# Routing on the unscaled residual sum, a quiet start of the experts, and a last scatter in four column pieces, in a two-layer transformer encoder

## The chip, the cores and the metric

The kernel runs on one core of a Trainium2 chip. The metric is the device time of one execution in microseconds, lower is better; it is given as the median of several runs. Names of engines: PE (TensorE matmul), PEld (its weight loads), DVE (VectorE), ACT (ScalarE), POOL (GpSimd), SP (SyncE, which here only issues DMAs).

## The reference

Two sequences (512 prompt tokens and 1024 sample tokens, width 1024, float32) go through the same two-layer encoder. A layer adds an attention mixer to the residual, and then a routed mixture of experts. What matters here is everything between the mixer's output projection and the experts' sum:

```python
x = x + concat(attention outputs) @ w_out          # residual sum, called y below
h = x * rsqrt(mean(x*x) + 1e-6) * gain             # norm before the experts
aff = softmax(h @ w_router, axis=-1)               # 16 experts
gates, idx = top_k(aff.T, 2 * tokens / 16)         # each expert picks its tokens
hid = silu(h[idx] @ w_gate) * (h[idx] @ w_up)
x = x.at[idx].add(gates * (hid @ w_down))          # scatter-add onto the residual
```

Each expert takes 64 prompt tokens and 128 sample tokens. All large products are made from a high and a low part (three matmuls of float32r in place of one of float32).

## The kernel before, in words

The program is a chain of phases with a barrier between each two: all engines finish a phase, SP's waits for its last stores among them, before any starts the next. Per layer: attention phases, then `output_phase` (L1055), then `expert_phase` (L1423). The output phase of the first layer also merges three attention parts (ME, `merge_start` and `merge_end`); that of the second does not.

**Output phase.** The 1536 tokens are 12 tiles of 128 rows, in the order of ORDER (eight sample tiles, then four prompt tiles). The loop runs over steps s; in step s each engine works on tile s - lag for each kind of work:

- lag 0: the loads, and the merge on DVE and ACT. lag 1: `turn_o` on PE (8 transposes), the copy to the high part on ACT (L1189) and the low part on DVE (L1268). lag 2: `multiply` on PE, 48 matmuls of 512 columns into the one accumulator ps_y; part 0 is the first half and waits for y_ready of the tile before, since ps_y must have been read.
- lag 3: DVE reads ps_y and adds the residual (yb, L1252, "the y add"), ACT squares and sums (L1195), POOL makes the reciprocal root (rstd, L1173 and L1174), DVE makes the normed tile hb (L1276), PE turns it (`turn_h`, L1325), ACT copies it out (L1211), PE multiplies it with the router weights (`route`, L1333).
- lag 4: DVE takes the row maximum (L1255), ACT the exponential (L1198), DVE the reciprocal and the product (L1261, L1265), PE turns the 16 affinities (`turn_a`, L1343), DVE copies them into the table aff (L1290). From the eighth tile on DVE runs rounds of `choose` (L1046; a round is MAX8, FIND_INDEX8 and MATCH_REPLACE8) on the sample rows: 3, 3 and 2 rounds behind the affinity copies of three steps.

Every engine works its list in program order. PE's list of a step is the order written at L1349: turn_o, multiply part 0, turn_h, turn_a, multiply part 1, route. DVE's list (L1245): y add, maximum, merge_start, reciprocal and product, low part, hb, merge_end, affinity copy, choose. SP stores y and h and waits at the end for the last stores (L1165).

**Expert phase.** DVE runs 8 more rounds of choose (`TopK.vector`, L1383), PE turns the lists, DVE makes gate and idx. Then POOL issues two indirect gathers (xs of 128 rows, xp of 64 rows, 4 KB each; L1527 and L1529). Weights come in 192 chunks of 1 MB over a ring of six buffers; SP issues the next load when DVE has made the low part of a chunk (`low`, L1592; three of them ahead of the first expert, LOOK = 3). DVE waits for `asked`, which POOL sets when both gathers are issued, then makes these three low parts, then takes part in splitting the turned tokens (`x_out`, L1597). The last four chunks of an expert are the down projection; DVE writes the scaled result of each into 256 columns of cs and cp (`result`, L1603). When the fourth is there POOL copies the index columns (L1513, L1514) and issues two indirect accumulating DMAs onto y (`add`, L1511, L1516 and L1518), and waits for them.

## Time and profile before

| what | value |
|---|---|
| median of 3 runs | 4049.76 us (4045.23 to 4051.99) |
| the profiled execution's own time | 4044.71 us |
| its span, first to last instruction | 4042.9 us |
| PE busy | 3810.6 us, 94% of the span |
| DVE / ACT / POOL busy | 2674.3 / 2134.8 / 859.5 us |
| mean granted TensorE clock | 0.973 of full speed |
| DMA | 583.89 MB, mean 144 GB/s |
| output phase, first layer | from 1194.3 to 1403.6 us of the span |
| output phase, second layer | from about 2870 to 3069.6 us |

Times in the rows below are microseconds from the span's start. In the timelines a row is start, duration, engine, line, operation, output <- inputs, count, and in brackets how long the engine had been idle before it and what released it. The duration of a matmul is longer than the distance to the next one, since matmuls overlap; distances between starts are what counts. A granted clock of 1.00 is 2.4 GHz and 0.50 is 1.2 GHz. PE is busy for almost the whole span, so time is found in the stretches where it isn't, or at the half clock: the joints between phases, and the step order of the output phase.

### The profile page before, as it was taken

Reading aid. Unit: us, or ns where it says so; the run is one execution under the profiler, and the core shown is the slowest. Engines: PE = TensorE matmul, PEld = TensorE weight load, DVE = VectorE, ACT = ScalarE, POOL = GpSimd, SP = SyncE. Lnnn points to the kernel's source line nnn. Section 1 sums busy time; section 2 is a strip of 40 time slices with the busy share of each in tenths; the row PEclk is TensorE's granted clock in tenths of the full one; section 3 lists DMA queues with packets and bytes.
Section 4 is the critical chain, followed back from the end, with each engine's and each line's share of the span. In section 5 each row is a group of like instructions: output and inputs, shape, how many; then the busy total and the mean of one; then the engine's idle time right before and its main releaser. Section 6 shows DMA issues by size and latency. Waiting matters only on the chain. (4 is left out here: it accounts for less than half of the span.)

```text
span 4042.9 us, 75073 instructions
## 1 busy us (share of the span) xinstructions
PE 3810.6 (94%) x27032; PEld 3679.2 (91%) x27032; DVE 2674.3 (66%) x5509; ACT 2134.8 (53%) x3992; POOL 859.5 (21%) x1437
## 2 busy tenths in 40 slices
PE   7999999999979879999999979999895999999998
PEld 7989988999978679999999979999785999999998
DVE  5665664667664567777777747777535777777775
ACT  5554554566642245656565546555322555656654
POOL 5132220444420011111111123333000111111110
PEclk9999999999989889999999989999997999999999
DMA  3000001122124378887788721000335778777884
GB/s 99 17 21 8 23 17 35 45 67 64 55 95 149 128 222 254 249 253 238 247 247 255 237 86 47 31 24 14 142 134 180 232 253 251 247 237 251 254 245 124
DMA packets 487368, 583.89 MB, mean 144 GB/s; under 512 B 18032, under 2 KB 442480, under 8 KB 487152
## 3 DMA queue, kind: packets, MB, share of 16 engines
q1 hardware_dynamic: 470640, 522.40, 39.3%
q0 software_dynamic: 14336, 50.34, 5.8%
q10 hardware_dynamic: 2176, 8.39, 0.5%
q8 instruction: 122, 2.00, 0.2%
q14 instruction: 94, 0.77, 0.1%
HBM read 514.85 MB, written 66.21 MB: 144 GB/s over the span
## 5 line engine op out<-in xcount | busy, mean ns | idle before, releaser
L1594 DVE TENSOR_TENSOR wl<-raw,wh 128x2048 fp32r<-128x2048 f32 x384 | 879.0, 2290 | 277.5 <-ACT wh L1549 276.7
L1549 ACT CAST wh<-raw 128x2048 fp32r<-128x2048 f32 x384 | 732.7, 1908 | 23.1 <-DMA raw<-in_w_gate 20.7
L1691 PE MATMUL ps_g<-xT,wh 128*128 128x384 f32 x2048 | 599.4, 359 | 3.2 <-DVE xT L1600 3.2
L1691 PE MATMUL ps_u<-xT,wh 128*128 128x384 f32 x2048 | 594.8, 357 | 0.0
L1693 PE MATMUL ps_g<-xT,wl 128*128 128x192 f32 x2048 | 479.0, 254 | 0.0
L1693 PE MATMUL ps_u<-xT,wl 128*128 128x192 f32 x2048 | 477.1, 253 | 0.0
L151 PE MATMUL psP<-ring_high,hTh 128*128 128x384 f32 (+1 forms) x1344 | 463.8, 345 | 11.9 <-ACT V L669 5.4
L152 PE MATMUL psP<-ring_low,hTh 128*128 128x384 f32 (+1 forms) x1344 | 445.1, 331 | 0.0
L153 PE MATMUL psP<-ring_high,hTl 128*128 128x384 f32 (+1 forms) x1344 | 445.0, 331 | 0.0
L1017 PEld LDWEIGHTS psO<-V,pT 128*128 128x128 f32 x3456 | 419.3, 192 | 18.9 <-issue 11.6
L1017 PE MATMUL psO<-V,pT 128*128 128x64 f32 x3456 | 415.9, 273 | 3.5 <-ACT pT L713 3.4
L1693 PEld LDWEIGHTS ps_g<-xT,wl 128*128 128x128 f32 x2048 | 388.6, 192 | 0.0
L1693 PEld LDWEIGHTS ps_u<-xT,wl 128*128 128x128 f32 x2048 | 385.8, 190 | 0.0
L1691 PEld LDWEIGHTS ps_g<-xT,wh 128*128 128x128 f32 x2048 | 378.6, 190 | 3.5 <-issue 3.5
L1691 PEld LDWEIGHTS ps_u<-xT,wh 128*128 128x128 f32 x2048 | 376.1, 189 | 0.0
L701 ACT ACTIVATE prob<-psS,nbias 128x384 f32<-128x384 f32 (+4 forms) x480 | 307.7, 647 | 77.4 <-DVE nbias L842 41.0
L713 ACT COPY pT<-psT 128x512 f32<-128x512 f32 (+2 forms) x348 | 182.7, 539 | 242.8 <-PE psT L1001 237.9
L613 POOL TENSOR_TENSOR xg<-xr,gains 128x256 f32<-128x256 f32 (+1 forms) x168 | 130.7, 778 | 781.2 <-ACT V L669 728.3
L1513 POOL COPY put_s<-idx 128x1 uint32 (+1 forms) x32 | 5.8, 182 | 1289.1 <-DVE cp L1613 1289.1
L151 PEld LDWEIGHTS psP<-ring_high,hTh 128*128 128x128 f32 x1344 | 256.4, 191 | 17.2 <-ACT V L669 8.6
L1001 PE MATMUL psT<-ident,prob 128*128 128x128 f32 x1728 | 244.7, 275 | 14.1 <-DVE pT L894 4.6
L152 PEld LDWEIGHTS psP<-ring_low,hTh 128*128 128x128 f32 x1344 | 256.6, 191 | 0.0
(198 smaller groups left out, 8679.2 us busy)
## 6 DMA issues: line engine op xcount, KB each, us to landing
raw<-in_w_gate SPq DMA_DIRECT2D x128, 1024.0 KB, 5.3
raw<-in_w_up SPq DMA_DIRECT2D x128, 1024.0 KB, 5.2
raw<-in_w_down SPq DMA_DIRECT2D x128, 1024.0 KB, 7.9
xb<-in_x SPq DMA_DIRECT2D x72, 256.0 KB, 2.8
out_y<-yb SPq DMA_DIRECT2D x24, 512.0 KB, 2.6
h_rows<-hb SPq DMA_DIRECT2D x24, 512.0 KB, 3.0
ring_raw<-in_w_a SPq DMA_DIRECT2D x24, 384.0 KB, 4.2
xb<-in_x SPq DMA_DIRECT2D x12, 512.0 KB, 4.4
```

What stands on the lines that cost most here:

```text
L151: eng.matmul(out, ah, bh, start=start, stop=False)
L152: eng.matmul(out, ah, bl, start=False, stop=False)
L153: return eng.matmul(out, al, bh, start=False, stop=stop)
L613: pool.tensor_tensor(xg[:, b, :], xr[:, b, :], gains[:, s, :], ALU.mult).then_inc(gained, 1)
L701: ins = act.activation(prob[:, u % 2, c * KC:c * KC + nk * P], psS[:, u % 2, c * 512:c * 512 + nk * P], ACT.Exp, bias=nbias[:, g % 4, x:x ...
L713: act.copy(pT[:, slot, at:at + w], room_of("R", u, k)[:, 0:w]).then_inc(pT_act, 1)
L1001: ins = pe.transpose(room_of("R", u, k)[:, x * P:(x + 1) * P], prob[:, u % 2, c * KC + j * P:c * KC + (j + 1) * P], ident)
L1017: ins = pe.matmul(psO[:, (off + c) * HD:(off + c + 1) * HD], pT[:, slot, at + x * P:at + (x + 1) * P], V[:, k0 + j, kv * HD:(kv + 1) * HD] ...
L1549: act.copy(wh[:, j % SPL], raw[:, j % RAW]).then_inc(w_high, 1)
L1594: dve.tensor_tensor(wl[:, j % SPL], raw[:, j % RAW], wh[:, j % SPL].bitcast(F32), ALU.subtract)\
L1691: both = lambda **fl: pe.matmul(ps[:, f, 0:2 * CAP], wh[:, j % SPL, k, fs], xT[:, k].rearrange("p h c -> p (h c)"), **fl)
L1693: high = lambda: pe.matmul(ps[:, f, 0:CAP], wl[:, j % SPL, k, fs], xT[:, k, 0, :], start=False, stop=False)
```

## The change

Three edits. The router's product is taken of y itself: the gain is multiplied into the router weights once (`wg`, on POOL), the root goes into the exponential as a scale per row (`lneg` is the maximum times the root), and the lag of routing falls from 4 to 3. PE turns y in place of hb; multiply is cut in four parts, with turn_y after the first, route after the second and turn_a after the fourth. hb (`scaled_tile`) is made off the router's chain, for the last tile after its affinity copy. The rounds of choose stand before the affinity copy of tiles 8, 9 and 10 instead of after that of 7, 8 and 9. In the expert phase DVE waits until both first gathers have landed before it makes its first low part, makes one, splits the tokens, then makes the other two; gate is written after idx. The last expert's scatter is issued in four pieces of 256 columns, each when its columns are ready.

```diff
-def output_phase(nc, state, o_parts, arec, x_rows, gain, w_router, ring, loaded, y_rows, h_rows, lists):
+def output_phase(nc, state, o_parts, arec, x_rows, gain, gain_col, w_router, ring, loaded, y_rows, h_rows, lists):
...
+            wait_alone(pool, router_in, 32, tally)
+            pool.tensor_tensor(wg[:, :, :], wr[:, :, :], spread(gc[:, :], 2, NE), ALU.mult).then_inc(gained, 1)
             for n in range(NT):
                 wait_alone(pool, squared, n + 1, tally)
                 chain.link(pool.tensor_scalar(ms[:, :], ss[:, :], 1.0 / D, EPS, ALU.mult, ALU.add))
-                pool.tensor_tensor(rstd[:, :], ms[:, :], half[:, :], ALU.pow).then_inc(rstd_ready, 1)
+                if n >= 2:
+                    wait_alone(pool, lexp, n - 1, tally)
+                    wait_alone(pool, h_ready, n - 1, tally)
+                pool.tensor_tensor(rstd[:, n % 2:n % 2 + 1], ms[:, :], half[:, :], ALU.pow).then_inc(rstd_ready, 1)
...
                     act.activation(sq[:, :], yb[:, n % 2, :], ACT.Square, accum_out=ss[:, :]).then_inc(squared, 1)
-                for n in at_step(s, 4):
-                    act.wait_ge(lmax_ready, n + 1)
-                    act.activation(le[:, :], ps_l[:, 0:NE], ACT.Exp, bias=lmax[:, :], scale=1.0,
-                                   accum_out=lsum[:, :]).then_inc(lexp, 1)
+                    act.wait_ge(y_turned, n + 1)
+                    if n >= 1:
+                        act.wait_ge(routed, n)
+                    act.copy(yT[:, :, :], ps_h[:, :, :]).then_inc(yT_out, 1)
...
                 for n in at_step(s, 3):
-                    act.wait_ge(h_turned, n + 1)
-                    if n >= 1:
-                        act.wait_ge(routed, n)
-                    act.copy(hT[:, :, :], ps_h[:, :, :]).then_inc(hT_out, 1)
+                    act.wait_ge(lmax_ready, n + 1)
+                    act.activation(le[:, :], ps_l[:, 0:NE], ACT.Exp, bias=lneg[:, :], scale=rstd[:, n % 2:n % 2 + 1],
+                                   accum_out=lsum[:, :]).then_inc(lexp, 1)
...
+            def scaled_tile(n):
+                b = n % 2
+                if n == 0:
+                    dve.wait_ge(const_in, 16)
+                dve.wait_ge(rstd_ready, n + 1)
+                if n >= 2:
+                    dve.wait_ge(h_st[b], 16 * (n // 2))
+                dve.scalar_tensor_tensor(hb[:, b, :], yb[:, b, :], rstd[:, b:b + 1], gb[:, :], ALU.mult, ALU.mult)\
+                   .then_inc(h_ready, 1)
+
...
                     b = n % 2
-                    dve.wait_ge(multiplied, 2 * n + 2)
+                    dve.wait_ge(multiplied, n + 1)
                     dve.wait_ge(x_in[b], 16 * (n // 2 + 1))
                     if n >= 2:
                         dve.wait_ge(y_st[b], 16 * (n // 2))
+                        dve.wait_ge(y_turned, n - 1)
                     dve.tensor_tensor(yb[:, b, :], ps_y[:, :], xb[:, b, :], ALU.add).then_inc(y_ready, 1)
...
-                for n in at_step(s, 4):
+                for n in at_step(s, 3):
+                    b = n % 2
+                    if n < NT - 1:
+                        scaled_tile(n)
+                    dve.wait_ge(routed, n + 1)
+                    dve.wait_ge(rstd_ready, n + 1)
+                    if n >= 1:
+                        dve.wait_ge(lexp, n)
+                    dve.tensor_reduce(lmax[:, :], ps_l[:, 0:NE], AX.X, ALU.max, negate=True).then_inc(max_order, 1)
+                    dve.wait_ge(max_order, n + 1)
+                    dve.tensor_tensor(lneg[:, :], lmax[:, :], rstd[:, b:b + 1], ALU.mult).then_inc(lmax_ready, 1)
+                    dve.wait_ge(lexp, n + 1)
+                    dve.reciprocal(lrec[:, :], lsum[:, :]).then_inc(recip_order, 1)
+                    dve.wait_ge(recip_order, n + 1)
+                    if n >= 1:
+                        dve.wait_ge(a_turned, n)
+                    dve.tensor_scalar(la[:, :], le[:, :], lrec[:, :], None, ALU.mult).then_inc(aff_ready, 1)
+                    if n == 2 * PT:
+                        dve.wait_ge(a_out, n)
+                    if 2 * PT <= n < 2 * PT + 3:
+                        done = 3 * (n - 2 * PT)
+                        choose(dve, chain, best, at, aff, slice(64, AFF_ROWS),
+                               range(EARLY + done, EARLY + min(done + 3, EARLY)))
                     dve.wait_ge(a_turned, n + 1)
                     if n == 0:
                         dve.wait_ge(cleared, 2)
                     dve.tensor_copy(aff_place(n), ps_a[0:NE, 0:P]).then_inc(a_out, 1)
-                    if n == 2 * PT - 1:
-                        dve.wait_ge(a_out, n + 1)
-                    if 2 * PT - 1 <= n < 2 * PT + 2:
-                        done = 3 * (n - 2 * PT + 1)
-                        choose(dve, chain, best, at, aff, slice(64, AFF_ROWS),
-                               range(EARLY + done, EARLY + min(done + 3, EARLY)))
+                    if n == NT - 1:
+                        scaled_tile(n)
...
-                for k in range(part * KD // 2, (part + 1) * KD // 2):
+                for k in range(part * KW, (part + 1) * KW):
...
-                ins.then_inc(multiplied, 1)
...
+                if part == WQ - 1:
+                    ins.then_inc(multiplied, 1)
+
+            def turn_y(n):
+                pe.wait_ge(y_ready, n + 1)
                 if n >= 1:
-                    pe.wait_ge(hT_out, n)
+                    pe.wait_ge(yT_out, n)
                 for k in range(KD):
-                    ins = pe.transpose(ps_h[:, k, :], hb[:, n % 2, k * P:(k + 1) * P], ident)
-                ins.then_inc(h_turned, 1)
+                    ins = pe.transpose(ps_h[:, k, :], yb[:, n % 2, k * P:(k + 1) * P], ident)
+                ins.then_inc(y_turned, 1)
...
-                    pe.wait_ge(const_in, 32)
-                pe.wait_ge(hT_out, n + 1)
+                    pe.wait_ge(gained, 1)
+                pe.wait_ge(yT_out, n + 1)
...
-                    ins = pe.matmul(ps_l[:, 0:NE], hT[:, k, :], wr[:, k, :], start=(k == 0), stop=(k == KD - 1))
+                    ins = pe.matmul(ps_l[:, 0:NE], yT[:, k, :], wg[:, k, :], start=(k == 0), stop=(k == KD - 1))
...
                 for n in at_step(s, 2):
                     multiply(n, 0)
                 for n in at_step(s, 3):
-                    turn_h(n)
-                for n in at_step(s, 4):
-                    turn_a(n)
+                    turn_y(n)
                 for n in at_step(s, 2):
                     multiply(n, 1)
                 for n in at_step(s, 3):
                     route(n)
+                for n in at_step(s, 2):
+                    multiply(n, 2)
+                    multiply(n, 3)
+                for n in at_step(s, 3):
+                    turn_a(n)
@@ TopK.vector
-        dve.tensor_copy(self.gate[:, 0:NE], cols[:, 0:NE])
         dve.tensor_copy(self.idx[:, 0:NE], cols[:, n:n + NE])
-        dve.tensor_tensor(self.gate[:, 32:32 + NE], va, vb, ALU.max)
...
         dve.tensor_tensor(self.idx[:, 32:32 + NE], ib, late[:, 2, :], ALU.add).then_inc(self.chosen, 1)
+        dve.tensor_copy(self.gate[:, 0:NE], cols[:, 0:NE])
+        chain.link(dve.tensor_tensor(self.gate[:, 32:32 + NE], va, vb, ALU.max))
@@ expert_phase, gpsimd
+            def add_by_chunk(e):
+
+                for c in range(NCH):
+                    pool.tensor_scalar(piece_s[:, c:c + 1], idx[:, e + 32:e + 33], float(NCH), float(c), ALU.mult, ALU.add)
+                    ins = pool.tensor_scalar(piece_p[:, c:c + 1], idx[0:CAP_P, e:e + 1], float(NCH), float(c), ALU.mult, ALU.add)
+                ins.then_inc(pool_order, 1)
+                wait_alone(pool, pool_order, 2 * NE, tally)
+                pieces = y_rows.rearrange("t (c f) -> (t c) f", f=FC)
+                for c in range(NCH):
+                    cols = slice(c * FC, (c + 1) * FC)
+                    wait_alone(pool, scaled, NCH * e + c + 2, tally)
+                    pool.indirect_dma_start(pieces, bass.IndirectOffsetOnAxis(ap=piece_s[:, c:c + 1], axis=0), cs[:, cols],
+                                            None, compute_op=ALU.add).then_inc(s_added, 16)
+                    pool.indirect_dma_start(pieces, bass.IndirectOffsetOnAxis(ap=piece_p[:, c:c + 1], axis=0), cp[:, cols],
+                                            None, compute_op=ALU.add).then_inc(p_added, 16)
+                wait_alone(pool, s_added, 16 * (e + NCH), tally)
+                wait_alone(pool, p_added, 16 * (e + NCH), tally)
...
-            add(NE - 1)
+            add_by_chunk(NE - 1)
@@ expert_phase, vector
-            dve.wait_ge(asked, 1)
-            for j in range(LOOK):
+            dve.wait_ge(xs_in, 16)
+            dve.wait_ge(xp_in, 16)
+            low(0, 0)
+            x_out(0)
+            for j in range(1, LOOK):
                 low(0, j)
-            x_out(0)
```

## Rows read from the trace of the kernel before

**Rows 1.** Windows: busy time by engine, granted clock, DMA share, GB/s.

```profile
1239.00:1341.00 102.00, 102.00 (x557) 86.45 (x557) 50.05 (x105) 24.02 (x49) 5.19 (x14) 1.00 0.47 164
...
1375.50:1379.00 3.50, 3.44 (x9) 2.70 (x10) 1.68 (x3) 1.34 (x4) 0.74 (x2) 0.54 0.38 150
```

**Rows 2.** Timeline of PE in the first output phase, around two tile changes.

```profile
1224.04 0.39 PE L153 MATMUL ps_y<-wh,oTl 128*128 128x512 f32 x1
...
1225.84 0.47 PE L151 MATMUL ps_y<-wh,oTh 128*128 128x512 f32 x1 [0.54 <-DVE yb L1252]
...
1296.92 0.40 PE L153 MATMUL ps_y<-wh,oTl 128*128 128x512 f32 x1
...
1298.85 1.07 PE L1307 MATMUL ps_t<-ident,ob 128*128 128x128 f32 x8
...
1299.68 0.47 PE L151 MATMUL ps_y<-wh,oTh 128*128 128x512 f32 x1
```

**Rows 3.** Timeline of DVE, the y adds: tiles 0, 1, 8, 9, 11; second layer 8, 11.

```profile
1224.47 1.22 DVE L1252 TENSOR_TENSOR yb<-ps_y,xb 128x1024 f32<-128x1024 f32 x1 [6.49 <-PE ps_y L153]
...
1238.18 1.22 DVE L1252 TENSOR_TENSOR yb<-ps_y,xb 128x1024 f32<-128x1024 f32 x1 [5.60 <-PE ps_y L153]
...
1341.72 1.22 DVE L1252 TENSOR_TENSOR yb<-ps_y,xb 128x1024 f32<-128x1024 f32 x1 [3.98 <-PE ps_y L153]
...
1359.10 1.23 DVE L1252 TENSOR_TENSOR yb<-ps_y,xb 128x1024 f32<-128x1024 f32 x1
...
1389.60 1.22 DVE L1252 TENSOR_TENSOR yb<-ps_y,xb 128x1024 f32<-128x1024 f32 x1 [1.02 <-issue]
...
3009.14 1.22 DVE L1252 TENSOR_TENSOR yb<-ps_y,xb 128x1024 f32<-128x1024 f32 x1 [5.32 <-PE ps_y L153]
...
3055.62 1.23 DVE L1252 TENSOR_TENSOR yb<-ps_y,xb 128x1024 f32<-128x1024 f32 x1 [1.01 <-issue]
```

**Rows 4.** Timeline of PE and DVE: an affinity turn and its copy.

```profile
1367.02 0.27 PE L1347 MATMUL ps_a<-ident,la 128*16 128x128 f32 x1
...
1367.33 0.28 DVE L1290 COPY aff<-ps_a 16x128 f32<-16x128 f32 x1 [2.78 <-PE ps_a L1347]
```

**Rows 5.** Timeline of DVE: start of the first three rounds of choose.

```profile
1352.56 0.69 DVE L1050 MAX8 best<-aff 48x8 f32<-48x512 f32 x1
```

**Rows 6.** Timeline of DVE and PE at the end of the first output phase.

```profile
1393.06 1.28 DVE L1276 SCALAR_TENSOR_TENSOR hb<-yb,rstd,gb 128x1024 f32<-128x1024 f32 x1 [0.34 <-POOL rstd L1174]
...
1394.40 1.97 PE L1330 MATMUL ps_h<-ident,hb 128*128 128x128 f32 x8 [3.20 <-DVE hb L1276]
```

**Rows 7.** Waits of SP's queue, 1390 to 1410 us: total, times, longest.

```profile
SPq L1165 <- DMA h_rows<-hb: 2.2, 1, 2.2
```

**Rows 8.** Timeline of POOL and PE at the start of the first layer's experts.

```profile
1425.22 3.27 POOL L1527 DMA_INDIRECT xs<-h_rows,idx  x1 [32.19 <-DVE idx L1406]
1428.79 1.56 POOL L1529 DMA_INDIRECT xp<-h_rows,idx  x1 [0.30 <-issue]
...
1442.04 0.98 POOL L1506 DMA_INDIRECT xs<-h_rows,take_s  x1 [0.79 <-POOL take_p L1504]
1443.32 0.91 POOL L1508 DMA_INDIRECT xp<-h_rows,take_p  x1 [0.30 <-issue]
```

**Rows 9.** DMA issues, 1425 to 1450 us: us from issue to landing.

```profile
xp<-h_rows,idx POOLq DMA_INDIRECT x1, 8.0
...
xp<-h_rows,take_p POOLq DMA_INDIRECT x1, 4.6
```

**Rows 10.** Timeline of DVE and POOL at the end of the span.

```profile
4028.07 0.34 DVE L1613 TENSOR_SCALAR cp<-yp,gate 64x256 f32<-64x256 f32 x1
...
4029.68 1.58 POOL L1516 DMA_INDIRECT out_y<-cs,put_s  x1 [0.81 <-POOL put_p L1514]
4031.57 1.44 POOL L1518 DMA_INDIRECT out_y<-cp,put_p  x1 [0.30 <-issue]
```

**Rows 11.** DMA issues, 4020 us to the end: us from issue to landing.

```profile
out_y<-cp,put_p POOLq DMA_INDIRECT x1, 5.6
```

More of the change, by code:

```diff
@@ L1268, in _ @@
                     dve.tensor_tensor(oTl[:, n % 2], ps_t[:, :, :], oTh[:, n % 2].bitcast(F32), ALU.subtract).then_inc(ol_out, 1)
-                for n in at_step(s, 3):
-                    b = n % 2
-                    if n == 0:
-                        dve.wait_ge(const_in, 32)
-                    dve.wait_ge(rstd_ready, n + 1)
-                    if n >= 2:
-                        dve.wait_ge(h_st[b], 16 * (n // 2))
-                    dve.scalar_tensor_tensor(hb[:, b, :], yb[:, b, :], rstd[:, :], gb[:, :], ALU.mult, ALU.mult)\
-                       .then_inc(h_ready, 1)
                 if ME:
@@ L1285, in _ @@
                     w_low(3)
-                for n in at_step(s, 4):
+                for n in at_step(s, 3):
[21 more added lines that the diff above has]
+                               range(EARLY + done, EARLY + min(done + 3, EARLY)))
                     dve.wait_ge(a_turned, n + 1)
@@ L1354, in _ @@
                 for n in at_step(s, 3):
-                    turn_h(n)
-                for n in at_step(s, 4):
-                    turn_a(n)
+                    turn_y(n)
                 for n in at_step(s, 2):
@@ L1461, in expert_phase @@
     joined, scaled = ph.sem("joined"), ph.sem("scaled")
[L1462 removed]
+    pool_order, tally = ph.sem("pool_order"), ph.sem("tally")
     XB = 3
@@ L1757, in moe @@
                 lists = (aff[:, :], best[:, :], at[:, :])
-                output_phase(nc, state, o_parts, rec, x_in, a["gain_ffn"][layer], a["w_router"][layer],
+                output_phase(nc, state, o_parts, rec, x_in, a["gain_ffn"][layer], a["gain_ffn_col"][layer], a["w_router"][layer],
                              kept, loaded, y_rows, h_rows, lists)
@@ L1818, in lay_out @@
         "gain_b": gains(i["qn_b"][0], i["kn_b"][0], B_NQ), "gain_c": gains(i["qn_c"][0], i["kn_c"][0], C_NQ),
+        "gain_ffn_col": np.stack([np.ascontiguousarray(x.reshape(KD, P).T) for x in i["norm_ffn"]]),
         "sink": rows(i["sink_c"][0]), "w_out_ab": i["w_out_ab"][0], "w_out_c": i["w_out_c"][0],
```

38 lines of the change are left out of this document (15 added, 23 removed).

## The prediction

> **What bounds it now.** The busy shares say that PE has work nearly all the time, so I went to the joints and to the step order, stage by stage. First the windows: through the middle of the first output phase PE is busy for 102.00 of 102.00 us at a granted clock of 1.00 [rows 1]. The timeline of PE shows why: between the last matmul of a tile and the first of the next it has a route (1.70 us) and turn_o (0.83 us) to do, 2.76 us from start to start [rows 2], and under that DVE empties ps_y. Where there was no route yet, at 1224.04, the same change took 1.80 us and PE idled 0.54 us until the y add had ended. So ps_y is a single accumulator, and the gap is the larger of PE's own filling and the y add's chain. The timeline of DVE gives the pace: tiles 1 to 8 are 14.79 us apart (103.54 / 7), tiles 8 to 11 take 47.88 us, in the second layer 46.48 us, because rounds of choose make the y add late [rows 3]. After the last tile comes a serial chain (hb, turn, copy, route, affinities) [rows 6], then the selection, the first gathers, and, at each layer's end, the last scatter. In these stretches PE waits, and every microsecond counts.
>
> **The step order, per tile.** Taken out of the gap: route. Put in its way: DVE. DVE's list now ends a step with the affinity copy of tile s-3, which waits for turn_a, and PE reaches turn_a only behind the fourth part of multiply. The y add stands behind that copy. From the last matmul's start L: turn_a starts at about L + 0.3 (an estimate, the 0.23 us pitch of matmuls and a short load), the copy 0.31 later, 0.28 long [rows 4], so the y add starts at L + 0.95 instead of L + 0.43 (1224.47 - 1224.04) [rows 2, 3]. From its start to the next tile's matmul it is 1.37 us (1225.84 - 1224.47), so the gap is 2.3 us. PE fills only turn_a and 0.83 us of turn_o of it. The route returns inside multiply at 1.70 us. Period: 14.79 - 2.76 + 2.3 + 1.70 = 16.0 us, 1.25 more a tile. Bounds: 0.1, if PE's fillers cover the gap, and 2.7, if in every gap the clock fell as well (below). I take 1.25, all its parts being measured here.
>
> Tile 0 to 1: no route stood behind tile 1's multiply before; now one stands inside, with 0.08 to restart, and the y add is 0.52 later: +2.3. Tiles 1 to 8: 7 x 1.25 = +8.7. The other work fits: the turn of y needs only the y add, the copy of yT is over 2 us before the route, affinities are ready some 3 us before turn_a, and SP, whose load of x is queued behind the store of the later hb, still has most of a step for it. POOL's new waits on lexp and h_ready are for tile n - 2 and long met; its multiplication of the router weights lies under the first steps. The extra maximum-times-root is 0.2 us a tile on DVE, under multiply: 0.
>
> **Choose.** Three rounds take 6.54 us (1352.56 to 1359.10) [rows 3, 5]. They now stand before the affinity copy, and can't start before the product of the tile: route ends 10.5 us after L, in the first layer DVE is then held by the merge and hb to about 12.9, in the second to about 12.1. Then 6.54: the y add is late by 2.8 us (first layer) or 2.0 (second) at tile 9, and by 2.0 at tile 10; two rounds fit. The gaps of PE there are 4 to 5 us. Before, a gap that held a route and an idle 1 us was followed by 0.54 of full clock for 3.5 us [rows 1], 1.2 GHz for most of it; I add 1.2 us for each of the two (0 if the clock holds, 1.7 at most). Tiles 8 to 11: 3 x 16.03 + 2.8 + 2.0 + 2.4 = 55.3 against 47.9, and 54.5 against 46.5: +7.4 and +8.0.
>
> **The tail.** The last y add ends at 1390.82, the turn of h starts 3.58 later, after square, root and hb [rows 3, 6]. The turn of y starts 0.2 later: -3.4, and +0.2 for the added product. But the last hb now comes behind the last affinity copy: 1.28 us, SP's issue 0.32, and SP then waits for the landing as it did before, 2.2 us [rows 7], only that now the barrier waits with it: +3.9. Together +0.7 a layer (between -3.2, if the barrier didn't wait for it, and +1.5).
>
> Output phases: 2.3 + 8.7 + 7.4 + 0.7 = 19.1 and 19.7, **+38.8**.
>
> **The first gathers.** POOL's issue of xs took 3.27 us and of xp 1.56 while DVE made three low parts; the next two, with DVE idle, 0.98 and 0.91 [rows 8]. The first xp landed 8.0 us after its start, at 1436.8, beside weight loads; the later one in 4.6 [rows 9]. Now DVE is silent and with it SP, whose loads wait for low parts. The indices come 0.17 us sooner (two writes fewer ahead of them): 1425.05 + 1.28 (distance of the two issues, 1443.32 - 1442.04) + 4.6 = 1430.9, 5.9 sooner. One low part now stands before the tokens' split and delays it by about 0.5; the other two follow under PE's first chunk of 7 us. So -5.4 a layer, **-10.8**; bounds 0 and -12, and -7.6 if issue and landing were as in the quiet last scatter (1.89 apart, 5.6 to land) [rows 10, 11]. Here the Trainium skill differs: "SBUF — State Buffer", in "Who interferes with whom", states that a DVE operation with two SBUF inputs and GpSimd's reads exclude each other for a whole instruction, and calls this lock the only cause of contention. By that rule alone only the issues shorten, 2.9 us a layer, and the sum below would be 5 us higher. The trace bears out the issues, but from the issue's end to the landing it also shows 6.4 us against 3.7.
>
> **The last scatter.** The columns are complete at 4028.41. xs starts 1.27 later, xp another 1.89, and lands 5.6 after its start, 4037.2 [rows 10, 11]. Now three of four pieces are gone by then (two issues of 1.6 us in 4.8 us of matmuls), and the index copies are done long before. Start of s at +0.5, of p at +2.4. Of the 5.6 its issue of 1.44 stays; the rest, 4.2, moves a quarter of the bytes: between 1.05 and 4.2, I take 2.6. Landing at 4028.41 + 2.4 + 4.0 = 4034.8, 2.4 sooner, and 2.5 with rounding; two layers, **-5** (bounds -1.5 and -8). The Trainium skill, "DMA: Bandwidth & Descriptors", "Bandwidth", calls transfers under 64 KB bound by their descriptors; the piece of xp is just 64 KB. By its fit in "Anatomy of one DMA" (2.0 us and the bytes at 436 GB/s) it would be an estimated 2.2 us instead of 4.0, and the sum 3.6 us lower. No run shows it yet.
>
> **Sum.** +38.8 - 10.8 - 5 = +23.0 on the profiled execution's 4044.7 us: 4067.7. The median shown stands 5.1 us above that execution, so I add half, 2.5: about **4070 us**. What this kernel's measurement can tell from no change is 0.2%, 8 us.
>
> **Rivals.**
> 1. The y add isn't held by the affinity copy, but still bounds the gap: 0.52 less for 22 tile changes, -11: 4059. It would need turn_a to run ahead; PE's list is against it, no row for it. 0.12.
> 2. The other side, faster: PE's fillers cover the y add, place ps_y's release, so that the gap stays under 1.3 us from start to start and route inside multiply costs nothing. That gives back 1.15 in each of 20 gaps (-23), the clock drops at choose with them (-4.8) and turn into 4070 - 28 = 4042, and with the quiet gathers at the far bound (-1.2) and the pieces at theirs (-3) 4038. It decides from that distance on. Against it is the 1.80 us at 1224.04, where nothing held DVE. 0.08.
> 3. The clock falls in every tile: a gap of 2.3 us with 1.4 of idleness, 1.3 us more in 20 gaps: 4096. For it: the fall shown followed an idle 1 us. Against: the gaps of 2.76 us never did it in 102 us [rows 1]. 0.07.
> 4. The gathers aren't quicker, since not the memory's other traffic but their rows' own latency sets them, or since the late low parts take it back: +5 to +11, 4075 to 4081. For it: nothing before shows a first gather alone. 0.11.
> The forecast has the rest, 0.62, by itself 4060 to 4080.
>
> **Range.** 4052 to 4084 takes in the forecast, rivals 1 and 4 and the bounds of gathers and scatter, and leaves out 2 and 3. Faster than 4041.7: 0.08. Within 8 us: 0.10, from the lower half of rival 1 and a forecast with all gains at their far ends. Slower: 0.82.
>
> **What would show it.** Y adds 16.0 us apart in tiles 1 to 8, each with the affinity copy just before it, and PE idle about 1.4 us before each tile's first matmul, released by yb. In each layer two longer gaps at choose with a clock of 0.5 behind them. A turn of y 0.2 us after the last y add, and SP's wait for h_rows directly before the next phase. xs and xp issued in about 1 us, landing near 1431 in the old timing, first expert matmul 5 us sooner after the indices. After the last column piece some 6.4 us to the landing instead of 8.8. The prediction is wrong if the y adds stay under 15.2 us apart.

## The result, and the profile after

The changed kernel takes 4071.0 us (median of 4 runs, 4068.58 to 4074.41), the kernel before 4049.85 us (4 runs, 4045.23 to 4051.99): ratio 1.0061, 95% interval 1.0049 to 1.0073, so 0.6% slower. The forecast was 4070, in a range of 4052 to 4084. The profiled execution has a span of 4070.3 us, where before had 4042.9.

The windows view of after, the stretch of [rows 1] and then the two stretches behind the first layer's choose gaps and the one behind the second gap of the second layer (columns: busy time of PE, PEld, DVE, ACT and POOL with their instructions, granted clock, DMA share, GB/s):

```profile
1239.00:1341.00 102.00, 95.85 (x517) 79.66 (x516) 48.13 (x101) 23.90 (x45) 5.19 (x14) 1.00 0.44 154
1371.50:1378.00 6.50, 5.76 (x16) 4.52 (x17) 3.01 (x3) 1.15 (x2) 0.74 (x2) 0.52 0.42 159
1392.00:1398.50 6.50, 5.71 (x16) 4.48 (x17) 1.93 (x2) 1.15 (x2) 0.74 (x2) 0.52 0.39 161
...
3075.00:3081.00 6.00, 5.21 (x12) 4.03 (x13) 1.93 (x2) 1.15 (x2) 0.74 (x2) 0.50 0.36 145
```

PE lost its full row: 6 of 102 us are idle at a full clock. Where rounds of choose stand the clock falls to half as well. Before had 3.5 us at 0.54 [rows 1]; now it is twice 6.5 us at a mean of 0.52 in the first layer.

The timeline of after around one ordinary tile change, to set beside [rows 2 to 4]:

```profile
1303.38 0.39 PE L153 MATMUL ps_y<-wh,oTl 128*128 128x512 f32 x1
...
1303.61 0.27 PE L1365 MATMUL ps_a<-ident,la 128*16 128x128 f32 x1
1303.71 1.04 PE L1324 MATMUL ps_t<-ident,ob 128*128 128x128 f32 x8
1303.91 0.28 DVE L1311 COPY aff<-ps_a 16x128 f32<-16x128 f32 x1 [3.86 <-PE ps_a L1365]
1304.23 1.22 DVE L1270 TENSOR_TENSOR yb<-ps_y,xb 128x1024 f32<-128x1024 f32 x1
...
1305.60 0.47 PE L151 MATMUL ps_y<-wh,oTh 128*128 128x512 f32 x1 [0.85 <-DVE yb L1270]
```

One line after another it is the chain that the prediction gave: last matmul, affinity turn, its copy, y add, next matmul. The gap is 2.22 us (1305.60 - 1303.38), and PE idles for 0.85 of it. The y adds stand 15.93 us apart in nearly all ordinary tiles, against 14.79. Then the choose tiles (timeline of DVE, then of PE):

```profile
1364.02 0.69 DVE L1050 MAX8 best<-aff 48x8 f32<-48x512 f32 x1
...
1370.56 0.28 DVE L1311 COPY aff<-ps_a 16x128 f32<-16x128 f32 x1
1370.87 1.23 DVE L1270 TENSOR_TENSOR yb<-ps_y,xb 128x1024 f32<-128x1024 f32 x1
```

```profile
1367.76 0.93 PE L1324 MATMUL ps_t<-ident,ob 128*128 128x128 f32 x7
1372.24 0.76 PE L151 MATMUL ps_y<-wh,oTh 128*128 128x512 f32 x1 [3.56 <-DVE yb L1270]
```

The three rounds run from 1364.02 to 1370.54, the product's last matmul was over by 1368, and the first matmul behind the gap already takes 0.76 us, not 0.47. From the y add of tile 8 to that of tile 11 it is 58.0 us (1352.23 to 1410.25), and 56.0 us in the second layer.

The end of the phase, the gathers and the scatter (timelines of DVE, SP and POOL):

```profile
1419.70 0.28 DVE L1311 COPY aff<-ps_a 16x128 f32<-16x128 f32 x1 [0.48 <-PE ps_a L1365]
1419.90 1.26 DVE L1258 SCALAR_TENSOR_TENSOR hb<-yb,rstd,gb 128x1024 f32<-128x1024 f32 x1
1421.19 0.32 SPq L1148 DMA_DIRECT2D h_rows<-hb  x1
...
1424.93 0.17 DVE L1409 MEMSET atf<- 112x128 f32 x1 [3.77 <-PEq L1123]
...
1446.43 1.26 POOL L1567 DMA_INDIRECT xs<-h_rows,idx  x1 [32.54 <-DVE idx L1425]
1447.99 0.92 POOL L1569 DMA_INDIRECT xp<-h_rows,idx  x1 [0.30 <-issue]
...
1458.66 0.68 PE L1732 MATMUL ps_g<-xT,wh 128*128 128x384 f32 x1 [1.58 <-DVE xT L1639]
...
4057.98 0.34 DVE L1652 TENSOR_SCALAR cp<-yp,gate 64x256 f32<-64x256 f32 x1
4059.11 1.56 POOL L1558 DMA_INDIRECT out_y<-cs,piece_s  x1 [1.51 <-DVE cp L1652]
4060.98 1.43 POOL L1560 DMA_INDIRECT out_y<-cp,piece_p  x1 [0.30 <-issue]
```

From the issue of xs to the first expert matmul it is 12.2 us where before had 17.0 (1425.22, in [rows 8], to 1442.26). From the end of the last cp to the end it is 12.0 us, before 14.5 (4042.9 - 4028.41, [rows 10]).

The tail of the output phase, from the last y add to the next phase, is not alike in the two layers: 14.68 and 12.57 us, where before had 13.95 in both. The timeline of PE shows where they differ, the router's product of the last tile:

```profile
1414.26 3.60 PE L1358 MATMUL ps_l<-wg,yT 128*128 128x16 f32 x16 [1.10 <-ACT yT L1207]
...
3096.26 1.96 PE L1358 MATMUL ps_l<-wg,yT 128*128 128x16 f32 x16 [1.10 <-ACT yT L1207]
```

The same 16 matmuls, after the same wait, take 3.60 us at a granted clock of 0.50 in the first layer and 1.96 us at 0.98 in the second. Before had 3.60 in both.

The ledger, by the profiled executions. "Output" runs from a layer's first y add to the first instruction of the expert phase on DVE; "gathers" from the issue of xs to the first expert matmul; "scatter" from the end of the last cp to the next phase or the end.

```
us, layer 1 / 2      before             after              change
output            179.1 / 177.7     200.3 / 195.9     +21.2 +18.3 = +39.5
gathers            17.0 /  17.1      12.2 /  11.7      -4.8  -5.4 = -10.2
index sooner                                           -0.2  -0.2 =  -0.3
scatter            14.4 /  14.5      11.9 /  12.0      -2.5  -2.5 =  -5.0
sum                                                             = +24.0
span             4042.9            4070.3                         +27.4
```

The missing 3.4 us can be placed in the attention phase between the layers (514.9 us before, 518.9 after, and between 516 and 520 in the runs below), where the change touches nothing. The medians differ by 21.2 us. Up to its first y add the program varied by 6 us from run to run (1221.5 to 1227.6). So a part's gain is read from its own stretch, not from the total alone.

### The profile page after: what moved, and what is told of

Its sections match the earlier page's. It is cut to its first block and busy times, and to the rows that moved or that the text cites. A ratio compares the mean times of both kernels' runs of the same rounds, so it can differ in the third digit from the quotient of the medians.

```text
span 4070.3 us, 75220 instructions
## 1 busy us (share of the span) xinstructions
PE 3819.6 (94%) x27032; PEld 3681.3 (90%) x27032; DVE 2679.3 (66%) x5533; ACT 2139.6 (53%) x3992; POOL 895.4 (22%) x1463
## 5 line engine op out<-in xcount | busy, mean ns | idle before, releaser
L787 DVE TENSOR_REDUCE ss<-xn 128x4 f32<-128x256 f32 (+1 forms) x168 | 73.5, 438 | 279.5 <-ACT xn L676 266.1
```

## The experiments

All times are medians; the ratios are against runs of before on the same chip, shared by each group of kernels. Before had there 4047.2, 4047.4 and 4046.45 us in the three groups. "After" itself was not run beside them, so where a run is set against it, the stretches of the ledger decide; each comes from one profiled execution.

### 1. The old output phase with the new gathers and scatter

```diff
-def output_phase(..., gain, gain_col, w_router, ...):   # after
+def output_phase(..., gain, w_router, ...):             # before, whole
```

> The output phase of before, with the changed gathers and the changed last scatter. My theory (the output phase costs about 39 us, the gathers give 10.8 and the scatter 5): 4050 - 16 = about 4034, and the y adds stand 14.79 us apart as in before. Rival, that the loss is not in the output phase but in what the router weights or the shorter gathers do elsewhere: above 4050. Rival, that the gathers are not quicker by themselves: about 4045.

4027.41 us, ratio 0.9953 (0.9939 to 0.9967). The y adds are 14.79 us apart again, and the output stretch is that of before to 0.1 us (179.1 and 177.7). Gathers are 11.9 and 11.9 us, scatter 12.0. By the stretches this is 15.4 us less than before. The medians differ by 19.8, with an interval of 13 to 25; in the profiled executions 2.0 us of it stand ahead of the first y add. So the new output phase as a whole (the router's place, the rounds and the last hb) carries the loss, and the other two edits together are a gain.

### 2. The affinity turn before the last part of multiply

```diff
     for n in at_step(s, 2):
         multiply(n, 2)
-        multiply(n, 3)
     for n in at_step(s, 3):
         turn_a(n)
+    for n in at_step(s, 2):
+        multiply(n, 3)
```

> After, with the transpose of the affinities moved from behind part 4 of the multiply to between parts 3 and 4. My theory (y add waits for that transpose and the copy of it, 0.5 us of each ordinary tile): period of an ordinary tile 15.93 - 0.5 = 15.4, some 8 ordinary tiles of each layer, so 4071 - 8 to 10 = 4061 to 4063; the three tiles with choose rounds keep their 18 to 20 us, since there the rounds end after the multiply. Rival, that the copy never held the add (it only waits for the product): same time as after, 4071, period 15.93.

4060.46 us, ratio 1.0034 (1.0021 to 1.0048). Timeline of PE and DVE at a tile change of this run:

```profile
1302.50 0.40 PE L153 MATMUL ps_y<-wh,oTl 128*128 128x512 f32 x1
...
1302.94 1.23 DVE L1270 TENSOR_TENSOR yb<-ps_y,xb 128x1024 f32<-128x1024 f32 x1 [2.52 <-PE ps_y L153]
...
1304.31 0.47 PE L151 MATMUL ps_y<-wh,oTh 128*128 128x512 f32 x1 [0.54 <-DVE yb L1270]
```

The add now waits for the product itself and starts 0.44 us behind the last matmul's start instead of 0.85, and the gap is 1.81 us, the 1.80 of [rows 2]. So the copy did hold the add, but for 0.41 us. The period falls by only 0.31, to 15.62, since the turn now stands inside the multiply. What is left of the loss is the add itself: PE still idles 0.54 us a tile. Of the 12.1 us that the two output stretches win, 5.2 stand ahead of tile 8. In the first layer 4.0 come from the choose tiles and 2.0 from the tail, where the clock fell less or not at all (last section), and 1.0 from the second layer's choose tiles.

### 3. The last hb in its ordinary place

```diff
-                    if n < NT - 1:
-                        scaled_tile(n)
+                    scaled_tile(n)
...
-                    if n == NT - 1:
-                        scaled_tile(n)
```

> After, with the last tile's scaled h made in its ordinary place, before the row maximum, instead of behind the last copy of the affinities. My theory (the store of h_rows ends last before the barrier, 2.2 us behind the last copy): the end of the output phase 3 to 4 us sooner in each layer, 4071 - 7 = about 4064. Rival, that the affinities' own chain ends last: same as after, or up to 1 us a layer longer because the 1.26 us of the scaling stands ahead of the maximum.

4061.09 us, ratio 1.0037 (1.0023 to 1.0050). Timeline of DVE at the end of this run's first output phase:

```profile
1415.99 1.28 DVE L1258 SCALAR_TENSOR_TENSOR hb<-yb,rstd,gb 128x1024 f32<-128x1024 f32 x1 [2.46 <-POOL rstd L1182]
...
1421.81 0.28 DVE L1310 COPY aff<-ps_a 16x128 f32<-16x128 f32 x1 [0.48 <-PE ps_a L1362]
1423.03 0.17 DVE L1406 MEMSET atf<- 112x128 f32 x1 [0.94 <-PEq L1123]
```

hb lies under the turn and route of y, where DVE has nothing to do, and the barrier comes 1.2 us behind the affinity copy, not 5.2 (1424.93 - 1419.70). From the last y add to the next phase it is 10.7 and 8.8 us, against 14.7 and 12.6: 4.0 and 3.8 less. "Off the router's chain" had put the instruction at the end of DVE's list, and a store behind it.

### 4. The rounds of choose before the row maximum

```diff
+                    (the rounds of choose)
                     dve.wait_ge(routed, n + 1)
                     dve.wait_ge(rstd_ready, n + 1)
...
-                    (the rounds of choose)
                     dve.wait_ge(a_turned, n + 1)
```

> After, with the three choose rounds of tiles 8, 9 and 10 moved from between the affinities and their transpose's copy to before the row maximum, where VectorE otherwise idles until the router has multiplied; nothing else changed. My theory (the rounds push the affinity copy and the y add past the end of the multiply): tiles 8 to 11 from 58.0 and 56.0 us back to 48 to 50, so 4071 - 15 to 18 = 4053 to 4056. Rival, that the rounds cost what VectorE lacks in all, wherever they stand: 56 to 58 again in the first layer, where the merge of branch A also runs, about 4065 to 4071.

4053.78 us (11 runs), ratio 1.0018 (1.0008 to 1.0027). In the second layer tiles 8 to 11 are ordinary: 15.83, 15.79, 15.79 us. In the first, where branch A's merge fills DVE too, two of three still are late (19.01, 18.59, 15.80): 53.4 us. The output stretches fall by 5.4 and 8.6 us. Place is the cause in the second layer. In the first it is place for nearly half (4.6 of the 10.2 us over three ordinary tiles). The two late tiles that remain have two causes. At the first (19.01 us) the rounds start late: merge and hb end at 1360.1, the three rounds run from 1360.18 to 1366.68, and PE waits 3.02 us for the affinities. At the second (18.59 us) the rounds hold nothing, as the timeline of DVE and a windows view show:

```profile
1387.01 0.28 DVE L1311 COPY aff<-ps_a 16x128 f32<-16x128 f32 x1 [4.41 <-PE ps_a L1365]
```

```profile
1370.00:1376.00 6.00, 6.00 (x16) 4.73 (x17) 4.52 (x7) 1.36 (x3) 0.74 (x2) 0.50 0.43 168
```

DVE has been idle for 4.41 us when the copy comes. Those 2.66 us over an ordinary tile are the half clock behind the first gap.

### 5. The three moves together

```diff
+    turn_a(n)             # between multiply(n, 2) and multiply(n, 3), as in 2
+    scaled_tile(n)        # in its ordinary place, as in 3
+    choose(...)           # before the row maximum, as in 4
```

> After, with three moves together and nothing else: the affinity transpose between parts 3 and 4, the choose rounds before the row maximum, the last scaled h in its ordinary place. If the three losses are separate, their gains add: 0.31 us in each of 8 ordinary periods of a layer, about 7.5 us for the last h, 13 to 17 for the choose rounds: 4071 - 26 to 30 = 4041 to 4045; period 15.62, tiles 8 to 11 near 47 us in the second layer. What is then left against the old output phase (4027) is the y add itself, some 0.8 us a tile. Rival, that they are one and the same wait seen three times: 4053, no better than the choose rounds moved alone.

4046.39 us (11 runs), ratio 0.9999 (0.9989 to 1.0008): as fast as before, and just above what I expected. The gains don't add. One y add of the first layer came 22.86 us after the one before it. Timeline of PE in it:

```profile
1365.87 0.38 PE L1362 MATMUL ps_a<-ident,la 128*16 128x128 f32 x1 [5.82 <-DVE la L1306]
```

With choose before the maximum the affinities are late, and with turn_a between parts 3 and 4 the multiply is queued behind them: PE stood 5.82 us in the middle of a product. Each move is safe by itself; together one makes the other's wait matter. The stretches: output 189.8 and 183.5 us, 10.5 and 12.4 less than after, where the three alone gave 34.9 in sum (12.1, 8.8 and 14.0; the first gains by a clock that did not fall, see the last section).

### 6. The gathers undone in the changed kernel

```diff
...
-            dve.wait_ge(xs_in, 16)
-            dve.wait_ge(xp_in, 16)
-            low(0, 0)
-            x_out(0)
-            for j in range(1, LOOK):
+            dve.wait_ge(asked, 1)
+            for j in range(LOOK):
                 low(0, j)
+            x_out(0)
```

> After, with the gathers of before: three low parts on VectorE before anything of the tokens, and not held back until the gathers land. My theory (the first gathers alone gain 5 us a layer): 4071 + 10 = 4081, with POOL's issue of xs back at 3.3 us and xp's landing at 8.0. Rival, that the gathers are quicker for another cause (the sooner index, the barrier's place): same as after, 4071.

4074.12 us, ratio 1.0069 (1.0056 to 1.0083): not the 4081 expected. The stretch is 14.1 and 13.6 us, so with the new order kept the wait is worth 1.9 us a layer, not 5. This run had kept the order of idx and gate, which I had taken for 0.17 us. Its timeline of DVE and POOL:

```profile
1443.43 4.56 DVE L1634 TENSOR_TENSOR wl<-raw,wh 128x2048 fp32r<-128x2048 f32 x2
1443.47 1.26 POOL L1567 DMA_INDIRECT xs<-h_rows,idx  x1 [32.47 <-DVE idx L1425]
1445.02 1.56 POOL L1569 DMA_INDIRECT xp<-h_rows,idx  x1 [0.30 <-issue]
```

The issue of xs takes 1.26 us beside a busy DVE, where in [rows 8] it took 3.27. In before it began 0.15 us after the first low part (1425.22 against 1425.07), here 0.04. That asked for the next three runs.

### 7. A busy DVE on a quiet memory

```diff
+            for j in range(LOOK):
+                low(0, j, early)       # SP is told later
+            dve.wait_ge(early, LOOK)
             dve.wait_ge(xs_in, 16)
             dve.wait_ge(xp_in, 16)
-            low(0, 0)
+            dve.sem_inc(w_low, LOOK)
             x_out(0)
-            for j in range(1, LOOK):
-                low(0, j)
```

> After, with VectorE making the three low parts of the weights right behind the choice, during the first gathers, but telling SP of them only once both gathers have landed, so that no weight load runs beside them: a busy VectorE on a quiet memory. From the issue of xs to the first expert matmul: after 12.2 and 11.7 us; with the low parts made and told of at once (the run that undid the wait) 14.1 and 13.6. If VectorE's work slows the gathers' issue and nothing else does: some 13.5 here. If the weight loads on the same memory slow them: xp lands in 4.7 us instead of 6.9, and since the first x low part no longer waits behind a weight's low part, 11.4 to 11.7, so the time is that of after or 0.5 to 1 us less.

4072.79 us, ratio 1.0066 (1.0052 to 1.0080). The stretch is 13.9 and 13.8 us. The timeline of DVE and POOL, and of the DMA issues, us to landing:

```profile
1444.28 6.70 DVE L1633 TENSOR_TENSOR wl<-raw,wh 128x2048 fp32r<-128x2048 f32 x3
1444.39 3.31 POOL L1567 DMA_INDIRECT xs<-h_rows,idx  x1 [32.48 <-DVE idx L1425]
1447.99 1.56 POOL L1569 DMA_INDIRECT xp<-h_rows,idx  x1 [0.30 <-issue]
```

```profile
xs<-h_rows,idx POOLq DMA_INDIRECT x1, 6.7
xp<-h_rows,idx POOLq DMA_INDIRECT x1, 4.9
```

With no new weight load asked for (from 1445 to 1447 us the DMA engines move 2 GB/s) the issue of xs is back at 3.31 us: DVE's low part alone holds it. And xp lands in 4.9 us, of which its issue is 1.56; in run 6, with the same issue of 1.56 and the weight loads beside it, it took 7.1. So there are two effects, each worth about 2 us: VectorE's work on the issue, the loads on the landing. In this run it is only the first, in run 6 only the second; before had both. Their sum, 3.6 and 4.0 us, leaves 1.2 and 1.4 of before's 4.8 and 5.4 open. Part of it shows in the landings: from the end of its issue xp took 6.4 us in before (8.0 - 1.56), 5.5 in run 6 and 3.3 here.

### 8. Before with only the gate instructions moved; before with only the wait

```diff
-        dve.tensor_copy(self.gate[:, 0:NE], cols[:, 0:NE])
...
-        dve.tensor_tensor(self.gate[:, 32:32 + NE], va, vb, ALU.max)
...
         dve.tensor_tensor(self.idx[:, 32:32 + NE], ...).then_inc(self.chosen, 1)
+        dve.tensor_copy(self.gate[:, 0:NE], cols[:, 0:NE])
+        chain.link(dve.tensor_tensor(self.gate[:, 32:32 + NE], va, vb, ALU.max))
```

> Before, with nothing changed but the place of the two 0.17 us gate instructions: behind the index instead of ahead of it (and the dummy activation reads another tile, so that it has nothing to wait for). My theory (VectorE's first low part starts 0.15 us ahead of the issue of xs in before and keeps it at 3.27 us; 0.1 to 0.15 us of delay lets the issue go first, as in the run that undid the wait): issue of xs 1.2 us, xs to first matmul 14.0 instead of 17.0 us, so 4047 - 6 = about 4041. Rival, that the order of the two is of no effect on the issue and the difference lies elsewhere in the changed kernel: 17.0 us again, 4047.

4039.27 us (11 runs), ratio 0.9985 (0.9976 to 0.9994). The timeline shows the issue at 1.26 us again, 0.03 us behind the low part:

```profile
1427.48 4.56 DVE L1594 TENSOR_TENSOR wl<-raw,wh 128x2048 fp32r<-128x2048 f32 x2
1427.51 1.26 POOL L1527 DMA_INDIRECT xs<-h_rows,idx  x1 [32.02 <-DVE idx L1404]
```

The wait alone, in before's kernel:

```diff
...
-            dve.wait_ge(asked, 1)
-            for j in range(LOOK):
+            dve.wait_ge(xs_in, 16)
+            dve.wait_ge(xp_in, 16)
+            low(0, 0)
+            x_out(0)
+            for j in range(1, LOOK):
                 low(0, j)
-            x_out(0)
```

> Before, with only the wait changed: VectorE makes no low part until both gathers have landed; the gate instructions stay ahead of the index. My theory: 11.9 to 12.2 us from the issue of xs to the first matmul instead of 17.0, index 0.15 us later than in the changed kernel, so 4047 - 10 = about 4037. Rival, that wait and order each give a part and add up (wait alone 15 us, -4): 4043.

4034.68 us (6 runs), ratio 0.9968 (0.9956 to 0.9980). Its timeline of POOL:

```profile
1427.55 1.26 POOL L1527 DMA_INDIRECT xs<-h_rows,idx  x1 [32.18 <-DVE idx L1406]
1429.11 0.92 POOL L1529 DMA_INDIRECT xp<-h_rows,idx  x1 [0.30 <-issue]
```

The runs together:

```
                                 xs to first matmul, layer 1 / 2
before                              17.0 / 17.1
gates behind the index (8)          14.0 / 13.9
wait for the landings (8)           11.9 / 11.8
both (1)                            11.9 / 11.9
both, in after                      12.2 / 11.7
```

The two don't add: 3.1 and 5.2 alone, 5.2 together. The wait takes all of it and makes the order idle; without the wait, a delay of some 0.1 us of DVE is worth 3 us.

### 9. The scatter undone

```diff
...
-            add_by_chunk(NE - 1)
+            add(NE - 1)
```

> After, with the last expert's rows scattered whole, as before. My theory (pieces of a quarter row take 2.5 us off each layer's end): 4071 + 5 = 4076; from the last scaled piece of cp to the next phase or the end 14.4 us, where after has 11.9. Rival, that the piecewise scatter only shifts a wait into the next phase's first loads: 4071.

4074.47 us, ratio 1.0067 (1.0053 to 1.0081). Timeline and DMA issues at its end:

```profile
4062.44 0.33 DVE L1652 TENSOR_SCALAR cp<-yp,gate 64x256 f32<-64x256 f32 x1
...
4065.93 1.44 POOL L1540 DMA_INDIRECT out_y<-cp,put_p  x1 [0.30 <-issue]
```

```profile
out_y<-cp,put_p POOLq DMA_INDIRECT x1, 5.4
```

14.4 us behind the first layer's last cp (after 11.9) and 14.2 at the end (12.0), so the pieces give 2.2 to 2.5 us a layer. The attention phase behind it was not quicker for the old form (519.5 against 518.9 us, both in the spread of 516 to 520), so nothing is seen to be only shifted.

### 10. The product in halves

Here the accumulator's two banks are released one by one: from tile 1 on multiply takes all k of columns 0 to 511, then all k of 512 to 1023; the y add is cut in the same two halves, the first while the second half is multiplied. The turn of the affinities, the last hb and the rounds stand as in the diff below.

```diff
-    dve.tensor_tensor(yb[:, b, :], ps_y[:, :], xb[:, b, :], ALU.add).then_inc(y_ready, 1)
+    cs = slice(c * 512, c * 512 + 512)
+    dve.tensor_tensor(yb[:, b, cs], ps_y[:, cs], xb[:, b, cs], ALU.add).then_inc(y_ready, 1)
...
+    steps = [(k, part // 2) for k in range(part % 2 * KD // 2, (part % 2 + 1) * KD // 2)]
...
+                    scaled_tile(n)
+                    choices(n, 0)       # 1 round
                     dve.wait_ge(routed, n + 1)
...
+                    choices(n, 1)       # 1, 2, 2 rounds
                     dve.wait_ge(a_turned, n + 1)
                     dve.tensor_copy(aff_place(n), ps_a[0:NE, 0:P]).then_inc(a_out, 1)
+                for n in at_step(s, 2):
+                    add_half(n, 0)
```

> After, with the multiply ordered by column half (k inside) from tile 1 on, the y add in two halves, the first during the second half of the multiply, the transpose of the affinities between parts 3 and 4, the choose rounds spread before the maximum and behind the affinities (2, 3 and 3 a tile), and the last scaled h in its ordinary place. My theory (what after lost is the accumulator held by the y add and by what stands before it): TensorE never waits for the add, period 14.8 to 15.1 in all tiles, also those with choose rounds (before 14.79 and 15.1 to 17.4), the end of the phase 9 to 11 us behind the last y add (before 13.95); with 4027.4 for the old output phase and the same gathers and scatter, 4027 - 2 x (1 to 2 + 3 to 5) = 4013 to 4022. Rival, that VectorE's sum of work is the bound where rounds are chosen: 17 to 19 us in those tiles of the first layer, about 4025 to 4030.

4022.78 us, ratio 0.9942 (0.9928 to 0.9955). The windows view, and the timeline of PE and DVE at a tile change:

```profile
1239.00:1341.00 102.00, 102.00 (x557) 85.66 (x556) 53.12 (x118) 25.12 (x49) 5.25 (x14) 1.00 0.45 159
```

```profile
1296.67 0.40 PE L153 MATMUL ps_y<-wh,oTl 128*128 128x512 f32 x1
1296.90 1.04 PE L1330 MATMUL ps_t<-ident,ob 128*128 128x128 f32 x8
1297.10 0.69 DVE L1268 TENSOR_TENSOR yb<-ps_y,xb 128x512 f32<-128x512 f32 x1 [1.80 <-PE ps_y L153]
...
1297.70 0.48 PE L151 MATMUL ps_y<-wh,oTh 128*128 128x512 f32 x1
```

PE is busy for all of the 102 us again, and the next product starts 1.03 us after the last matmul's start, filled by turn_o alone, while the second half of the add still runs. The period is 14.84 us: with route inside multiply and no exposed add, that is before's 14.79 again. So the ordinary period's 1.14 us of loss is 0.78 of exposed add (15.62 - 14.84), 0.31 of the copy ahead of it, and 0.05 of the rest. The last tile gives what the change meant: 9.3 and 9.9 us from the last half add to the next phase, against 13.95. The time is just above the 4013 to 4022 that I expected, since tiles 8 to 11 did not come down to 14.8 to 15.1 us each: they take 15.7 on the mean of the first layer and 15.1 in the second, less than the 17 to 19 of the rival.

With one round of each tile moved behind the first half of the add:

```diff
                 for n in at_step(s, 2):
                     add_half(n, 0)
+                for n in at_step(s, 3):
+                    choices(n, 2)       # 1 round
```

> The version in halves, with one choose round of each tile moved behind the first half of the next y add, so that no round stands between the multiply's first half and the add of it. My theory: where rounds are chosen the multiply of the next tile starts 0.5 to 1 us sooner, 1 to 3 us in both layers together: 4019.5 to 4022 where the version before it took 4022.8. Rival, that the second half of the add, now behind that round, holds the turn of y and gives it back: 4022 to 4024.

4018.28 us (5 runs), ratio 0.9929 (0.9915 to 0.9942). Tiles 8 to 11 take 46.3 and 44.7 us instead of 47.0 and 45.3 (before 47.9 and 46.5). Their intervals overlap, so that it beats the version above is not shown; both beat before and after. The output stretches are 175.3 and 172.4 us, 25 and 24 less than after's.

## Why the prediction was right

**The step order.** Right in mechanism, 10% too dear. Period 16.0 forecast, 15.93 measured; the copy's hold was taken as 0.52 and is 0.41 (run 2), the rest of the chain as given. The idleness of about 1.4 us before each first matmul was wrong: it is 0.85, since turn_a and turn_o both lie in the gap. Tile 0 to 1: +2.3 forecast, +2.2 measured (15.92 - 13.71). Rival 1 (the copy doesn't hold the add) falls by the timeline, where the add starts 0.32 us after the copy, and by run 2.

**Choose.** Right in place and cause, too low in size: 55.3 and 54.5 us forecast, 58.0 and 56.0 measured. The step that failed is the clock term. I added 1.2 us for each of two gaps, from the 3.5 us at 0.54 of [rows 1], and gave 1.7 as its bound. The windows show 6.5 us at 0.52 behind each gap of the first layer, so at most 3.1 us (6.5 x 0.48). Where little but the clock differs it is 2.5 us (tile 9 to 10: 20.55 here, 18.02 in run 2, whose clock held) and 2.7 (run 4's second late tile, 18.59 against 15.93), beyond my bound. The lateness of the y add was nearly as forecast: 18.64 - 15.93 = 2.7 and 18.03 - 15.93 = 2.1 us at tile 9, against 2.8 and 2.0.

**The tail.** +0.7 forecast, +0.7 measured in the first layer (14.68 - 13.95), with SP's wait for h_rows at 2.2 us as before. In the second it was -1.4, and there the forecast is wrong: I had carried over before's router product of 3.60 us, which is one at the half clock, and the clock held there (1.96 us). Run 3 shows the late hb to cost the 3.9 I had given it.

**Output phases:** +38.8 forecast, +39.5 measured, closer than its terms, and that is luck. The choose tiles came out 4.2 us dearer in the two layers together (+10.1 and +9.5 against +7.4 and +8.0). The tiles up to the eighth came out 1.5 us cheaper and the second layer's tail 2.1.

**The gathers.** The size was right (-10.8 forecast, -10.5 with the sooner index), the reason not taken apart. I priced a quiet VectorE and a quiet memory together. Run 7 and run 6 separate them, at about 2 us a layer each. The Trainium skill, "SBUF — State Buffer", "Who interferes with whom", names the lock on the shared ports as the only cause of contention. For the landing that is not enough here: in run 6 the weight loads beside it add 2.2 us to xp's landing at an equal issue. The same section of the Trainium skill states that the order of issue decides who blocks. The traces agree as far as they can: the issue takes 1.26 us when it starts 0.03 us behind the low part (run 8) and 3.31 us when it starts 0.11 us behind it (run 7). But in both VectorE's start is the earlier one in the profile, so which of the two had the port first is not seen. What I missed altogether was that the gate's move alone would give 3 us a layer.

**The scatter.** -2.4 a layer forecast, -2.5 measured. The last piece lands 3.2 us after its start in the profile's row, where I had taken 4.0:

```profile
out_y<-cp,piece_p POOLq DMA_INDIRECT x1, 3.2
```

The Trainium skill's fit in "DMA: Bandwidth & Descriptors", "Anatomy of one DMA", gave an estimated 2.2. The measurement stands between the two. The pieces start a little later than I had them, s 0.8 us after the end of cp (4059.11 - 4058.32), not 0.5, and p 2.7, not 2.4, so the landing comes 5.9 us after the end of cp where I had 6.4; the end of the span follows 6.1 us behind it, not 5.7 as in before, and that takes most of this half microsecond back.

**The sum.** 4070 was forecast and 4071.0 measured. That it is so close is luck as well: the stretches give +24.0 us against a forecast of +23.0, the span +27.4 and the medians +21.2, and the 2.5 us that I added for before's median were half of a difference between its executions.

**Rivals 2, 3 and 4.** Rival 2 needed PE's fillers to cover the add; they did not. Run 10 shows that the add can be hidden by cutting it in two, and then, with the other moves of run 5, the kernel takes 4018 to 4023. Rival 3 (the clock falls in every tile) did not come about: 1.00 over the 102 us. Rival 4 (gathers no quicker) falls by runs 1 and 8.

## What to carry to other kernels

An instruction moved off a chain stands somewhere else in a list, and all that is queued behind it there inherits its waits: here an affinity copy ahead of the one instruction that releases a single accumulator, and a scaled tile ahead of a store and a barrier. Ask of each move what is the next instruction on that engine and who waits for it; two moves that are good alone can spoil each other (run 5). And a resource that is filled and emptied in turn is better split in two than guarded by the right order: halves of the accumulator took away the wait that three reorderings could only shorten.

## What the runs showed of the hardware

**A race of 0.1 us worth 3.** The indirect gather's issue on POOL takes 1.13 to 1.26 us where it begins 0.02 to 0.04 us after a VectorE operation with two SBUF inputs (both layers of runs 6 and 8), and 3.17 to 3.31 where it begins 0.09 to 0.15 us after it (both layers of before and of run 7); the difference, 2.0 us, is a little less than one such operation (2.29 us).

**The clock does not follow the length of the gap alone.** Before the tile behind the first choose gap of layer 1, PE waited 3.56 us in after and 3.57 us in run 2. Timeline rows of PE and windows, of run 2:

```profile
1369.82 0.47 PE L151 MATMUL ps_y<-wh,oTh 128*128 128x512 f32 x1 [3.57 <-DVE yb L1270]
```

```profile
1370.00:1376.00 6.00, 6.00 (x31) 4.97 (x31) 2.08 (x2) 1.87 (x3) 0.74 (x2) 1.00 0.53 188
1388.00:1394.00 6.00, 6.00 (x24) 4.87 (x24) 1.28 (x1) 1.55 (x3) 0.74 (x2) 0.72 0.44 178
```

There the clock stayed at 1.00, in after it had a mean of 0.52, which is the lower level, 1.2 GHz, for nearly all of the 6.5 us. Behind the second gap, 3.82 us in both runs, the clock fell in run 2 as well (0.72 over 6 us), but later. In run 4 a gap of 3.02 us ahead of the affinity turn and one of 0.71 us behind turn_o were followed by 6 us at 0.50. So run 2 won more in the choose tiles (18.02 us instead of 20.55 for tile 9 to 10) than its edit explains, and such a gap's price is a range: from nothing to about 2.7 us here. What decides it was not tried.
